# Convolution taps that read their input from PSUM, and one scan in place of four

## The chip, the core and the metric

The kernel runs on one core of a Trainium2 chip. The metric is the device time of one execution in microseconds, and lower is better. A span is the time from the first to the last recorded instruction of one profiled execution.

## What is computed

Two transformer blocks follow each other on one sequence of 512 tokens with 1024 channels, all in float32. The first block has a gated delta rule over four heads of 128; its q, k and v are projections of the normed input, put through a causal depthwise convolution of width 4 and SiLU:

```python
qkv = jax.nn.silu(causal_dwconv(jnp.concatenate([q, k, v], axis=-1), conv_w))   # width 4, zeros ahead of the first token
q, k, v = jnp.split(qkv.astype(jnp.float32), 3, axis=-1)
q = l2norm(q.reshape(hs))
k = l2norm(k.reshape(hs))
```

It ends with an MLP and a gated projection. The second block has an mLSTM over four heads beside a latent attention. The mLSTM's q and k come through a convolution of the same kind with a bias, and its forget gates through a log sigmoid and a running sum over the sequence:

```python
qk_ml = jax.nn.silu(causal_conv(qk_ml, conv_w, conv_b))                         # width 4
logf = jax.nn.log_sigmoid(chunk(f_pre).astype(f32))
b = jnp.cumsum(logf, axis=-1)
```

## The kernel before

Activations lie transposed, 128 channels on the partitions and 512 tokens along the free dimension, so a convolution over tokens is a sum of four shifted copies of a row, each times a number per partition. Every weight matrix is read in blocks of 128 by 1024 or the like. A block lands by DMA in one of three `raw` buffers; ScalarE writes its rounded upper part to `wh` (line 2325), GpSimd the residual to `wl` in two halves (line 1912), and TensorE multiplies each slice three times (`wh` and `wl` with the upper part of the activations, `wh` with their lower part, lines 1954 to 1956, or 984 to 986 where tokens lie on the partitions).

The order of all work is written out by hand. `plan()` lists the tiles; each is one GEMM into one of four PSUM banks, in turn. TensorE may start tile t when tile t - 4 has been read: it waits on `bank_read["act"]` or `bank_read["dve"]`, and `Plan.READER` says which engine counts for which kind of tile. Four more banks, `aux`, hold sums, transposes and small products. On ScalarE, `tile()` reads a tile and then splits the weight blocks whose slot is free by then (`split`); on VectorE, `tile()` waits for a GEMM, `freed` counts the bank as read, and `link` makes the next instruction wait for this one.

The first block's tiles are kn 0 to 3 (the keys), q 0 to 3, v 0 to 3, hp 0 and 1, ch 0 and 1, and so on. `HEADS` numbers the twelve convolutions: 0 to 3 keys, 4 to 7 q, 8 to 11 v. For keys, VectorE multiplies the tile by the norm factor into `craw` (`keys`, line 2705). For q and v, ScalarE copies the tile to `craw` (line 2429) and then writes the last tap to `cc` from the bank (line 2430), which frees it. VectorE adds the other three taps from `craw`, which has three zeros ahead of column 3 (`conv`, line 2750), and ScalarE applies SiLU (`conv_silu`, line 2439). `craw` and `cc` have two buffers each. Between the convolutions stand, on TensorE, the squared sums of the heads (line 2130) and the transposes of keys and v (line 2024); on VectorE, `kd` and `bv` (lines 2792 and 2804) read these transposes, and the `AT` tiles (line 2815) are made ahead of the gram matrices (lines 2168 and 2170), which wait for the last `bv`.

The second block begins with tiles gates2 and qk2 0 to 2, then v2 (0,0) to (0,3), qk2 3, and v2 (1,0) to (1,3). VectorE scales qk2 j by the norm factor `nrow` into `craw2` (`scaled_qk`), which frees the bank; ScalarE writes the last tap from `craw2` to `cc2`; VectorE adds three taps (line 1565). Between scaling and taps stand the forget gates: `lf`, four scans of 128 tokens each chained by their last column (line 1555), `nbs`, and later `c4`, the running maximum `m4` (line 1579), its splitting into `r4h` and `r4l`, and `em`. VectorE's order there is gates2, `scaled_qk(0)`, the forget gates, `ncol`, `scaled_qk(1)`, `conv(0)`, `scaled_qk(2)`, the maxima, `conv(1)`, `conv(2)`, `scaled_qk(3)`, `conv(3)`.

The functions that the diff touches, and what calls them:

## Time and profile before

| | |
|---|---|
| three runs | 1385.59, 1385.69, 1387.89 us; median 1385.69 |
| the profiled execution's own time | 1383.27 us |
| its span | 1381.5 us, mean granted TensorE clock 0.984 |
| TensorE busy | 1321.5 us (96%), 6265 matmuls |
| VectorE busy | 608.5 us (44%) |
| ScalarE busy | 527.0 us (38%) |
| GpSimd busy | 570.0 us (41%) |

Busy time is a share of the whole span, an average over stages with different limits. A matmul row's length is longer than the distance to the next one, since matmuls overlap; starts are the better ruler. Idle time of an engine other than TensorE says nothing by itself; what counts is whether TensorE waits.

### The profile page before, as it was taken

The page shows a single profiled execution, that of the slowest core. Times are in us where ns is not written, and L with a number is a line of the kernel's source. Part 1 is how long each engine was busy: PE and PEld are TensorE (multiplying, and loading weights), DVE is VectorE, ACT ScalarE, POOL GpSimd, SP SyncE. Part 2 cuts the span into 40 slices and gives each one's busy share as a digit, 9 for nine tenths or more (in the row PEclk, how much of TensorE's full clock was granted, in tenths as well). Part 3 has the DMA queues.
Part 4 walks back from the last instruction along what each step waited for, and adds up shares of the span by engine and source line. Part 5 has one row for each costly group of instructions (what it writes and reads, how often), then busy time and mean ns, then how long its engine had stood idle before and what let it go on. Part 6 is the DMA issues. An engine that isn't in the chain of part 4 may idle for free.

```text
span 1381.5 us, 15973 instructions
## 1 busy us (share of the span) xinstructions
PE 1321.5 (96%) x6265; PEld 1050.3 (76%) x6265; DVE 608.5 (44%) x847; ACT 527.0 (38%) x814; POOL 570.0 (41%) x429
## 2 busy tenths in 40 slices
PE   7999889999999999999999999989989999999997
PEld 5768778787888888888887865555768888888886
DVE  4967652335115421121376546466468513314123
ACT  5585323535222222221354434545445313323232
POOL 4334232254554554554554342211326544444440
PEclk9999999999999999999999999999999999999998
DMA  6422101232333333333332231100214333333321
GB/s 185 145 57 74 38 16 33 60 107 75 116 92 94 104 92 106 93 93 87 111 92 79 75 74 48 46 16 31 61 46 128 101 92 95 104 92 95 103 61 61
DMA packets 211665, 113.29 MB, mean 82 GB/s; under 512 B 17204, under 2 KB 209536, under 8 KB 211336
## 3 DMA queue, kind: packets, MB, share of 16 engines
q1 hardware_dynamic: 210488, 109.32, 27.9%
q10 hardware_dynamic: 976, 2.90, 0.6%
q8 instruction: 50, 0.82, 0.2%
q14 instruction: 23, 0.19, 0.0%
q0 software_dynamic: 128, 0.07, 0.0%
HBM read 110.16 MB, written 2.11 MB: 81 GB/s over the span
## 4 chain that ended last, share of the span: by engine, by line
PE 82%; DVE 6%; ACT 3%; POOL 1%; issue 1%; DVEq 0%; ACTq 0%
PE bank L1954 21%; PE bank L1956 21%; PE bank L1955 21%; PE aux L2202 1%; PE aux L2218 1%; PE bank L1106 1%; PE aux L1122 1%; PE aux L2231 1%; PE aux L1035 1%; POOL wl L1912 1%; PE aux L1954 1%; PE bank L984 1%; PE aux L1047 1%; PE bank L2002 1%; PE bank L986 1%
## 5 line engine op out<-in xcount | busy, mean ns | idle before, releaser
L1912 POOL TENSOR_TENSOR wl<-raw,wh 128x512 fp32r<-128x512 f32 (+1 forms) x402 | 548.0, 1387 | 748.0 <-ACT wh L2325 747.9
L1954 PE MATMUL bank<-ah,wh 128*128 128x512 f32 x888 | 355.7, 401 | 6.1 <-ACT cc L2430 3.4
L2325 ACT CAST wh<-raw 128x1024 fp32r<-128x1024 f32 (+1 forms) x201 | 208.2, 1038 | 370.2 <-PE bank L1956 358.1
L1956 PE MATMUL bank<-al,wh 128*128 128x512 f32 x888 | 347.8, 392 | 0.0
L1955 PE MATMUL bank<-ah,wl 128*128 128x512 f32 x888 | 347.7, 392 | 0.0
L1954 PEld LDWEIGHTS bank<-ah,wh 128*128 128x128 f32 x888 | 168.1, 189 | 45.9 <-issue 10.5
L1956 PEld LDWEIGHTS bank<-al,wh 128*128 128x128 f32 x888 | 167.8, 189 | 35.5
L1955 PEld LDWEIGHTS bank<-ah,wl 128*128 128x128 f32 x888 | 168.0, 189 | 35.0 <-issue 1.5
L1954 PE MATMUL bank<-yh,wh 128*128 128x512 f32 x488 | 190.6, 391 | 0.1
L1956 PE MATMUL bank<-yl,wh 128*128 128x512 f32 x488 | 190.0, 389 | 0.0
L1955 PE MATMUL bank<-yh,wl 128*128 128x512 f32 x488 | 189.9, 389 | 0.0
L1954 PEld LDWEIGHTS bank<-yh,wh 128*128 128x128 f32 x488 | 91.6, 188 | 19.2 <-DVE yl L2623 0.5
L1956 PEld LDWEIGHTS bank<-yl,wh 128*128 128x128 f32 x488 | 91.6, 188 | 19.1
L1955 PEld LDWEIGHTS bank<-yh,wl 128*128 128x128 f32 x488 | 91.6, 188 | 18.8
L873 DVE TENSOR_TENSOR y<-bank,sg 128x512 f32<-128x512 f32 x22 | 15.2, 692 | 166.5 <-PE bank L1956 161.1
L1794 DVE CAST yh<-y 128x512 fp32r<-128x512 f32 x32 | 34.7, 1085 | 77.7 <-ACT y L1483 77.7
L1809 DVE TENSOR_TENSOR acc<-bank,acc 128x512 f32<-128x512 f32 x23 | 15.9, 692 | 99.3 <-PE bank L1956 99.3
L915 DVE TENSOR_TENSOR x<-bank,x 128x512 f32<-128x512 f32 x24 | 16.6, 692 | 97.7 <-PE bank L1956 97.7
L1479 ACT ACTIVATE rl<-bank 128x512 f32<-128x512 f32 x32 | 19.1, 598 | 92.6 <-PE bank L1956 90.6
L1795 DVE TENSOR_TENSOR yl<-y,yh 128x512 fp32r<-128x512 f32 x32 | 52.2, 1630 | 1.1
L804 ACT ACTIVATE sg<-bank 128x512 f32<-128x512 f32 x22 | 13.2, 599 | 95.5 <-PE bank L1956 90.7
L2750 DVE SCALAR_TENSOR_TENSOR cc<-craw,par,cc 128x512 f32<-128x512 f32 x36 | 36.8, 1028 | 4.7 <-ACT cc L2430 3.3
(452 smaller groups left out, 1645.8 us busy)
## 6 DMA issues: line engine op xcount, KB each, us to landing
raw<-in_w_up SPq DMA_DIRECT2D x54, 512.0 KB, 3.9
raw<-in_w_down SPq DMA_DIRECT2D x48, 512.0 KB, 4.1
raw<-in_w_in SPq DMA_DIRECT2D x39, 512.0 KB, 3.9
raw<-in_w_gate SPq DMA_DIRECT2D x22, 512.0 KB, 3.8
raw<-in_w_out SPq DMA_DIRECT2D x16, 512.0 KB, 3.8
raw<-in_ple_gate SPq DMA_DIRECT2D x8, 512.0 KB, 3.9
raw<-in_w_down SPq DMA_DIRECT2D x8, 384.0 KB, 3.3
xtok<-in_x SPq DMA_DIRECT2D x4, 512.0 KB, 5.2
```

The lines of the kernel that those rows point to most:

```text
L873: freed(nc.vector.tensor_tensor(y, ps, sg[:, i % 3, :], ALU.mult))
L915: freed(nc.vector.tensor_tensor(x[:, m, :], ps, x[:, m, :], ALU.add))
L1479: tile("up2", (c, j), lambda ps: nc.scalar.activation(rl[:, :], ps, ACT.Relu))
L1794: link(nc.vector.tensor_copy(yh[c % 2][:, j, :], y))
L1795: nc.vector.tensor_tensor(yl[c % 2][:, j, :], y, yh[c % 2][:, j, :].bitcast(F32), ALU.subtract).then_inc(y_ready[1], 1)
L1809: freed(nc.vector.tensor_tensor(acc[:, m, :], ps, acc[:, m, :], ALU.add))
L1912: nc.gpsimd.tensor_tensor(wl[pl.slot[b]][:, half], raw[b % RAW][:, half], wh[pl.slot[b]][:, half].bitcast(F32), ALU.subtract).then_inc(wl_ ...
L1954: nc.tensor.matmul(ps, h[:, c:c + P], mh[:, k, :], start=(n == 0), stop=False)
L1955: nc.tensor.matmul(ps, l[:, c:c + P], mh[:, k, :], start=False, stop=False)
L1956: last = nc.tensor.matmul(ps, h[:, c:c + P], ml[:, k, :], start=False, stop=(n == nk - 1))
L2325: nc.scalar.copy(wh[pl.slot[b]][:, 0:w], raw[b % RAW][:, 0:w]).then_inc(wh_ready, 1)
L2750: i = nc.vector.scalar_tensor_tensor(c[:, :], r[:, tap:tap + T], g_of("conv_qkv", 12 * tap + conv_tile(j)), c[:, :], ALU.mult, ALU.add)
```

## The change

For q and v, ScalarE's copy to `craw` goes; it only writes the last tap from the bank. VectorE's three taps read the bank, each on a shorter stretch (tap 2 from column 1 of `cc` on, tap 1 from column 2, tap 0 from column 3), in place of the zeros ahead of the row. VectorE frees the bank with the last tap, so q and v are in `READER` as VectorE's. Keys are as before.

In the second block VectorE multiplies each qk2 bank by `nrow` in place, ScalarE writes the last tap from the bank, VectorE's taps read the bank and the last one frees it; `craw2` and its zeros go. The four chained scans become one over 512 tokens: its state is the sum of `lf` and the state, then the minimum of that and `lf`, which leaves the running sum as it is because no `lf` is above zero.

```diff
--- before.py
+++ after.py
@@ -177,7 +177,7 @@
-    READER = dict(kn="dve", q="act", v="act", hp="act", ch="dve", cc="dve", cb="dve", z="act", wout="dve",
+    READER = dict(kn="dve", q="dve", v="dve", hp="act", ch="dve", cc="dve", cb="dve", z="act", wout="dve",
                   gate="act", up="dve", down="dve", proj="act", pgate="act", gates2="dve", qk2="dve", v2="act",
@@ -357,7 +357,6 @@
         mrn = sb("mrn", [P, T])
-        craw2 = [sb(f"craw2{i}", [P, 3 + T], at=offs["qf"] + i * 2080) for i in range(2)]
         cc2 = [sb(f"cc2{i}", [P, T], at=offs["qf"] + 4160 + i * 2048) for i in range(2)]
@@ -509,7 +508,6 @@
         cols_loaded = signal("cols_loaded")
-        pads_zero = signal("pads_zero")
         alog_exp = signal("alog_exp")
@@ -524,7 +522,6 @@
         pt_ready = signal("pt_ready")
-        pads2_zero = signal("pads2_zero")
         pos_loaded = signal("pos_loaded")
@@ -539,7 +536,7 @@
         em_ready = signal("em_ready")
-        conv2_done = signal("conv2_done")
+        qk_scaled = signal("qk_scaled")
         silu2_ready = signal("silu2_ready")
@@ -663,6 +660,12 @@
             return aux[k % 6] if k < 4 or k > 5 else bank[k - 2]
+        def convolved(eng, j):
+            if j < H:
+                eng.wait_ge(conv_done, j + 1)
+            else:
+                evacuated(eng, *HEADS[j])
+
         def conv_tile(j):
@@ -1261,15 +1264,15 @@
             def conv_evac(j):
                 if j >= 2:
-                    act.wait_ge(conv2_done, j - 1)
+                    evacuated(act, "qk2", j - 2)
                     act.wait_ge(silu2_ready, j - 1)
                 tile("qk2", j)
+                act.wait_ge(qk_scaled, j + 1)
+                nc.scalar.activation(cc2[j % 2][:, :], bank[pl.at["qk2", j] % NBANK][:, :], ACT.Copy,
+                                     scale=g_of("conv_w_2", 12 + j)).then_inc(last_tap, 1)
+
+            def conv_silu(j):
                 evacuated(act, "qk2", j)
-                nc.scalar.activation(cc2[j % 2][:, :], craw2[j % 2][:, 3:3 + T], ACT.Copy,
-                                     scale=g_of("conv_w_2", 12 + j)).then_inc(last_tap, 1)
-
-            def conv_silu(j):
-                act.wait_ge(conv2_done, j + 1)
                 dst = (q2 if j < 2 else k2)[:, j % 2, :]
@@ -1531,15 +1534,10 @@
         def vector_second(dve, link, tile, freed, lower, norm_fill, add_square):
-            for i in range(2):
-                nc.vector.memset(craw2[i][:, 0:3], 0.0).then_inc(pads2_zero, 1)
             def scaled_qk(j):
                 ps = tile("qk2", j)
-                if j >= 2:
-                    dve.wait_ge(conv2_done, j - 1)
-                    dve.wait_ge(last_tap, H + j - 1)
-                freed(nc.vector.tensor_tensor(craw2[j % 2][:, 3:3 + T], ps, nrow[:, :], ALU.mult))
+                nc.vector.tensor_tensor(ps, ps, nrow[:, :], ALU.mult).then_inc(qk_scaled, 1)
             ps = tile("gates2", 0)
@@ -1550,23 +1548,19 @@
             link(nc.vector.scalar_tensor_tensor(lf[:, :], g2[:, :], 0.0, lf[:, :], ALU.min, ALU.subtract))
-            for c in range(NC):
-                s = slice(c * P, (c + 1) * P)
-                link(nc.vector.tensor_tensor_scan(bs[:, s], ones[0:8, :], lf[:, s],
-                                                  bs[:, c * P - 1:c * P] if c else 0.0, ALU.mult, ALU.add))
+            link(nc.vector.tensor_tensor_scan(bs[:, :], lf[:, :], lf[:, :], 0.0, ALU.add, ALU.min))
             nc.vector.tensor_scalar(nbs[:, :], bs[:, :], -1.0, None, ALU.mult).then_inc(forget_sums_ready, 1)
             def conv(j):
-                r, c = craw2[j % 2], cc2[j % 2]
-                dve.wait_ge(pads2_zero, 2)
-                evacuated(dve, "qk2", j)
-                dve.wait_ge(last_tap, H + j + 1)
+                ps, c = bank[pl.at["qk2", j] % NBANK], cc2[j % 2]
+                dve.wait_ge(last_tap, 3 * H + j + 1)
                 for tap in (2, 1, 0):
-                    i = nc.vector.scalar_tensor_tensor(c[:, :], r[:, tap:tap + T], g_of("conv_w_2", 4 * tap + j),
-                                                       c[:, :], ALU.mult, ALU.add)
+                    late = 3 - tap
+                    i = nc.vector.scalar_tensor_tensor(c[:, late:T], ps[:, 0:T - late], g_of("conv_w_2", 4 * tap + j),
+                                                       c[:, late:T], ALU.mult, ALU.add)
                     if tap:
                         link(i)
-                i.then_inc(conv2_done, 1)
+                freed(i)
             dve.wait_ge(ncol_ps, 1)
@@ -2414,7 +2408,7 @@
                 if j >= 2:
-                    act.wait_ge(conv_done, j - 1)
+                    convolved(act, j - 2)
                     act.wait_ge(silu_ready, j - 1)
@@ -2425,13 +2419,12 @@
                 act.wait_ge(gemm_done, t + 1)
-                act.wait_ge(pads_zero, 1)
-                nc.scalar.copy(craw[j % 2][:, 3:3 + T], bank[t % NBANK][:, :])
-                tile(kind, h, lambda ps: nc.scalar.activation(cc[j % 2][:, :], ps, ACT.Copy, scale=tap))
+                nc.scalar.activation(cc[j % 2][:, :], bank[t % NBANK][:, :], ACT.Copy, scale=tap).then_inc(last_tap, 1)
+                tile(kind, h)
             def conv_silu(j):
                 kind, h = HEADS[j]
-                act.wait_ge(conv_done, j + 1)
+                convolved(act, j)
                 if kind == "v" and h >= 2:
@@ -2710,7 +2703,7 @@
             nc.vector.memset(pin[:, 0, 0:16], 0.0)
-            nc.vector.memset(pin[:, 1, 0:16], 0.0).then_inc(pads_zero, 1)
+            nc.vector.memset(pin[:, 1, 0:16], 0.0)
             dve.wait_ge(ab_ps, 1)
@@ -2742,17 +2735,20 @@
             def conv(j):
                 r, c = craw[j % 2], cc[j % 2]
-                if j < H:
-                    dve.wait_ge(last_tap, j + 1)
-                else:
-                    evacuated(dve, *HEADS[j])
+                ps = tile(*HEADS[j]) if j >= H else None
+                dve.wait_ge(last_tap, j + 1)
                 for tap in (2, 1, 0):
-                    i = nc.vector.scalar_tensor_tensor(c[:, :], r[:, tap:tap + T],
-                                                       g_of("conv_qkv", 12 * tap + conv_tile(j)), c[:, :],
+                    late = 3 - tap if j >= H else 0
+                    src = ps[:, 0:T - late] if j >= H else r[:, tap:tap + T]
+                    i = nc.vector.scalar_tensor_tensor(c[:, late:T], src,
+                                                       g_of("conv_qkv", 12 * tap + conv_tile(j)), c[:, late:T],
                                                        ALU.mult, ALU.add)
...
                         link(i)
-                i.then_inc(conv_done, 1)
+                if j < H:
+                    i.then_inc(conv_done, 1)
+                else:
+                    freed(i)
             def head_norm(j):
```

## Rows read from the trace of the kernel before

**Rows 1.** The page of the whole run, its part 1: busy us (share) x instructions.

```profile
PE 1321.5 (96%) x6265; PEld 1050.3 (76%) x6265; DVE 608.5 (44%) x847; ACT 527.0 (38%) x814; POOL 570.0 (41%) x429
```

**Rows 2.** TensorE's waits, whole run: us in total, times, longest us.

```profile
PE bank L1954 <- ACT cc L2430: 3.4, 1, 3.4
...
PE bank L1954 <- POOL wl L1912: 1.9, 1, 1.9
...
PE bank L984 <- POOL wl L1912: 1.0, 1, 1.0
```

**Rows 3.** The answers for lines 2750 and 2661: duration ns min/median/max, first and last start.

```profile
L2750 DVE SCALAR_TENSOR_TENSOR cc<-craw,par,cc x36: 715/752/1828, 52.3 to 117.4; 128x512 f32<-128x512 f32 x36
...
L2661 DVE SCALAR_TENSOR_TENSOR zl<-aux,par,zh x6: 741/747/752, 12.2 to 22.2; 128x512 fp32r<-128x512 f32 x6
```

**Rows 4.** Timeline of VectorE, first block: start us, us, line, operation, tiles, count.

```profile
55.32 2.32 DVE L2750 SCALAR_TENSOR_TENSOR cc<-craw,par,cc 128x512 f32<-128x512 f32 x3
...
87.97 3.20 DVE L2750 SCALAR_TENSOR_TENSOR cc<-craw,par,cc 128x512 f32<-128x512 f32 x3
...
114.35 3.79 DVE L2750 SCALAR_TENSOR_TENSOR cc<-craw,par,cc 128x512 f32<-128x512 f32 x3
...
119.62 0.68 DVE L2804 TENSOR_TENSOR bv<-aux,gT 128x512 f32<-128x512 f32 x1
```

**Rows 5.** Timeline of TensorE around the first GEMM of v.

```profile
70.06 0.47 PE L1954 MATMUL bank<-ah,wh 128*128 128x512 f32 x1 [3.36 <-ACT cc L2430]
...
73.25 0.63 PE L1956 MATMUL bank<-al,wh 128*128 128x512 f32 x1
73.67 0.50 PE L1954 MATMUL bank<-ah,wh 128*128 128x512 f32 x1
74.01 0.39 PE L1955 MATMUL bank<-ah,wl 128*128 128x512 f32 x1
```

**Rows 6.** Timeline of ScalarE ahead of it.

```profile
68.73 0.59 ACT L2429 COPY craw<-bank 128x512 f32<-128x512 f32 x1
69.22 0.69 ACT L2430 ACTIVATE cc<-bank,par 128x512 f32<-128x512 f32 x1
```

**Rows 7.** Timeline of TensorE, v 2 to the gram matrices.

```profile
90.67 0.58 PE L1954 MATMUL bank<-ah,wh 128*128 128x512 f32 x1 [1.85 <-POOL wl L1912]
...
118.85 1.03 PE L2024 MATMUL aux<-cst,vT 128*128 128x128 f32 x8
121.84 1.13 PE L2168 MATMUL aux<-kT 128*128 128x128 f32 x8 [1.95 <-DVE bv L2804]
```

**Rows 8.** Timeline of ScalarE ahead of v 2.

```profile
88.21 1.04 ACT L2325 CAST wh<-raw 128x1024 fp32r<-128x1024 f32 x1
```

**Rows 9.** Two windows: busy of PE, PEld, DVE, ACT, POOL, granted clock, DMA share, GB/s.

```profile
90.00:96.00 6.00, 5.33 (x16) 4.26 (x17) 5.93 (x7) 4.03 (x7) 4.21 (x4) 0.72 0.34 90
120.00:126.00 6.00, 4.16 (x26) 3.77 (x27) 5.08 (x15) 5.27 (x11) 0.00 (x0) 1.00 0.02 5
```

**Rows 10.** Timeline of VectorE, second block.

```profile
754.22 4.07 DVE L1555 TENSOR_TENSOR_SCAN bs<-ones,bs,lf 8x128 f32<-8x128 f32 x3
...
759.87 2.32 DVE L1565 SCALAR_TENSOR_TENSOR cc<-craw,par,cc 128x512 f32<-128x512 f32 x3
...
768.37 4.56 DVE L1565 SCALAR_TENSOR_TENSOR cc<-craw,par,cc 128x512 f32<-128x512 f32 x6
```

**Rows 11.** Timeline of TensorE, second block.

```profile
759.09 1.02 PE L970 MATMUL aux<-g,cst 8*4 8x512 f32 x2
...
767.61 0.28 PE L984 MATMUL bank<-wh,ah 128*128 128x256 f32 x1
...
774.20 0.47 PE L1954 MATMUL bank<-ah,wh 128*128 128x512 f32 x1 [0.67 <-ACT v L1287]
```

**Rows 12.** The chain that ended last, second block: start us, us, engine, tile, line.

```profile
775.15 0.94 ACT wh L2325
776.17 5.03 POOL wl L1912 x4
```

More of the change, by code:

```diff
@@ L1263, in conv_evac @@
                 if j >= 2:
-                    act.wait_ge(conv2_done, j - 1)
+                    evacuated(act, "qk2", j - 2)
                     act.wait_ge(silu2_ready, j - 1)
                 tile("qk2", j)
-                evacuated(act, "qk2", j)
-                nc.scalar.activation(cc2[j % 2][:, :], craw2[j % 2][:, 3:3 + T], ACT.Copy,
+                act.wait_ge(qk_scaled, j + 1)
+                nc.scalar.activation(cc2[j % 2][:, :], bank[pl.at["qk2", j] % NBANK][:, :], ACT.Copy,
                                      scale=g_of("conv_w_2", 12 + j)).then_inc(last_tap, 1)
             def conv_silu(j):
-                act.wait_ge(conv2_done, j + 1)
+                evacuated(act, "qk2", j)
                 dst = (q2 if j < 2 else k2)[:, j % 2, :]
```

## The prediction

> **What bounds the kernel now.** Read the page first: TensorE is busy for 96% of the span [rows 1]. So an edit off TensorE changes the time only where TensorE stands still, or where it is made to. Next comes the list of TensorE's waits, kept to the two places that the change touches [rows 2]: 3.4 us for ScalarE's `cc` before the GEMM of v 0, 1.9 us for a weight residual of GpSimd before v 2, and 1.0 us for one in the second block, beside one of 0.67 us before qk2 3 [rows 11]. The scans have no row there. Then the timelines of these stretches, to see what ends each wait and what would be late next.
>
> A GEMM takes one of four banks, so it waits until the tile four places back has been read. v 0 waits for q 0, v 1 for q 1, v 2 for q 2; in the second block, v2 (0,1) for qk2 0, v2 (0,2) for qk2 1, v2 (0,3) for qk2 2. The change moves the release of exactly these banks from the end of one read to the end of three taps on VectorE.
>
> **Price of a tap.** From SBUF, `cc` and pointer scalar, undisturbed: 752 ns median, and 2.32 us for three in a row [rows 3, 4]. The nearest row with one operand in PSUM and a pointer scalar is the `zl` operation, 747 ns [rows 3]. I take 2.32 us for three taps from PSUM; bounds are 2.2 us (a little shorter operand, 509 to 511 columns) and 2.5 us (an unseen PSUM start cost). The upper end also covers this: the Trainium skill, "VectorE: DVE Perf Modes", section "Rules for kernel authors", advises copying a matmul's output to SBUF first when many operations follow, and its errata section charges a PSUM source 62 cycles more than an SBUF one; by it, as an estimate, each hold would last 0.2 us longer and the sum below rise by about 0.4 us. The trace's 747 against 752 ns does not show that surcharge for two-input operations.
>
> Beside GpSimd the SBUF taps are dearer: the longest took 1828 ns [rows 3], and conv 11 needed 3.79 us for three [rows 4]. The operation with a PSUM operand has a maximum of 752 ns. So 2.32 us holds there too, a saving of 1.4 us for conv 11.
>
> **First block, v 0.** ScalarE now copies q 0 (from 68.73) and then scales it (69.22, 0.69 us, ends 69.91); TensorE starts at 70.06, 0.15 us later [rows 5, 6]. New: the copy goes, the scaling runs 68.73 to 69.42, the taps 69.45 to 71.77, TensorE starts at 71.92. That is 1.86 us late; what ScalarE saves (0.49 us) is inside it. After the present wait the matmuls start 0.43 us apart until 73.67, then 0.23 us: TensorE at 1.2 GHz, then at 2.4 GHz [rows 5]. If the slow stretch ends at the same instant, the longer wait takes the place of some slow matmuls: before, nine matmuls started ahead of 73.67, now (73.67 - 71.92) / 0.43 = four, and the other five cost 5 x 0.23 = 1.1 us. If it lasts as long after the restart as before, the delay stays 1.86. I take 1.5.
>
> **First block, v 2.** Everything up to the key transposes follows TensorE, so it moves by 1.5. conv 6 starts behind `kd` 0 and 1, at 87.97 [rows 4], new 89.47, and frees q 2's bank at 91.79; TensorE starts at 91.94 instead of 90.67 [rows 7], 1.27 late. What it waits for today, the cast at 88.21 and the residual behind it [rows 8], moves by 1.5 less two saved copies (0.98), by 0.5, and is no longer last. The weight wait goes and a bank wait comes. The clock is open here. Today nine matmuls are slow after a wait of 1.85, which costs 8 x 0.2 = 1.6 us (granted 0.72 of full speed from 90 to 96); a wait of 1.95 at 121.84 left it at 1.00 [rows 7, 9]. The new wait is about 1.6 us. If the clock stays up, TensorE gains at most the 1.27 back, for then the head sums wait for ScalarE's squares: these stand behind silu 7, so behind conv 7, which VectorE reaches after conv 6 and two more `kd` at about today's time.
>
> **First block, the gram matrices.** Today they wait for `bv` 3, on a chain of VectorE: conv 11, eight `AT` tiles, `bv` 2, four tiles, `bv` 3 [rows 4]. conv 11 1.4 us shorter looks like that gain, but `bv` 2 needs the transposes that TensorE starts at 118.85 [rows 7]; the first four end about 119.4, `bv` 2 starts at 119.62. So 0.3 us is gained, and the transposes are late next. First block in all: 1.27 - 0.3 = +1.0 with the slow clock, -0.3 without. The rows split evenly; I take +0.4.
>
> **Second block, the hold.** conv 0 ends at 759.87 + 2.32 = 762.2 [rows 10]; v2 (0,1), 24 matmuls of 0.12 us ahead of v2 (0,2), needs it at 764.7: hidden. conv 1 is queued behind the scaling of qk2 2, the `c4` copy, the maximum scan and the splitting of maxima, and starts at 768.37. It frees qk2 1's bank at 768.37 + 2.28 = 770.65, but v2 (0,2) starts at 767.61 today [rows 11]. It will start at 770.80, 3.19 late. conv 2 follows at once and ends at 772.9, when v2 (0,3) is not yet due: hidden. A wait of 3.2 us is like that of 3.4 us before v 0, behind which the clock fell; I take the same 1.6 us on top (bounds 0 and 3.2). v2 (0,3) then ends 4.8 us late. Of that some is given back: today the casts wait behind four v2 reads that are queued behind silu 2, so the next cast starts at 775.15 on the chain [rows 12], 1.6 us after the last v2 matmul; new it starts some 0.55 us after it. The chain from there (cast, four halves on GpSimd, v2 (1,0) at 781.24) moves as a whole: 4.79 - 1.05 = +3.7. With the clock up it is +2.1. The 0.67 us wait before qk2 3 [rows 11] is inside the same slack.
>
> The scaling in place writes PSUM, which no VectorE row of before does. Four operations, two of them (qk2 1, qk2 2) ahead of conv 1. The same multiplication into SBUF takes 0.69 us; I take that, with bounds of 0.6 and 1.7 us (the dearest contended 512-column rows are near this), so -0.2 to +2.0 on the path.
>
> **The scan and the rest.** Four scans, the last three of them 4.07 us [rows 10], become one over 512 columns. It is worth 3 to 4 us to VectorE, and nothing to the end: the next thing is the copy of `ncol`, which waits for TensorE's small matmuls behind the GEMM of qk2 2, and the matmuls that use the sums start at 759.09 without a wait [rows 11]. The cover is the qk2 2 GEMM; were it gone, the 3 to 4 us would count. If one scan took as long as four, nothing changes. The memsets of the pads, three columns each, and eight ScalarE copies (0.59 us each [rows 6]) lie beside GEMMs, but for the two already counted. No DMA is issued anew or moved past another; the weight ring follows the GEMMs. The new wait of VectorE for the GEMM is over before its `last_tap` wait is.
>
> **Sum.** +0.4 + 3.7 = +4.1 us. The profiled execution took 1383.27 us (span 1381.5) and would take 1387.4; the median of the runs shown is 1385.69, 2.4 us above it, and I forecast from that: 1389.8 us.
>
> **Rivals.**
> - A, the holds bind but the clock is kind (0.22): +2.1 in the second block, -0.3 to +0.4 in the first: +1.8 to +2.5, 1388. For it: the wait of 1.95 us that left the clock up. Against: the clock did fall after the waits of 3.4 and 1.9 us [rows 5, 9].
> - B, faster (0.06): VectorE's relief decides. If conv 1 ended by 767.5, 3.1 us before it is due by my rows, the second block would cost nothing, and the first could give 1.6 for the clock and 0.3 at the gram matrices: -1.9, 1383.8. It would take the maximum scan chain to start earlier, but it hangs on `ncol` and `cb_ps` of TensorE. A rule of the Trainium skill points this way: "SBUF — State Buffer", section "SBUF: two separate sides", has a VectorE operation with two SBUF inputs shut GpSimd out for its whole length, and the reverse. The long taps agree; but what is freed this way stands off TensorE's chain.
> - C, costlier (0.10): the in-place write or taps from PSUM are slow, or the clock is half for twice as long: +6 to +8, 1392 to 1393.5. For it: no such row. Against: `zl` at 747 ns.
> - The forecast (0.62): +2.8 to +6, 1388.5 to 1391.5.
>
> **How the numbers follow.** 0.2% is 2.8 us, about what a measurement of this kernel tells from no change. Slower by more: C and most of the forecast, with a little of A: 0.66. Within it: A and the low edge of the forecast: 0.28. Faster: B: 0.06. The range takes A's low end with the spread of the runs (1386.3) and C's near end (1392.8).
>
> **What would show it.** In the profile after: (1) a wait of about 5 us before v 0, ended by VectorE's tap; (2) before v 2 a bank wait in place of GpSimd's; (3) a new wait of about 3.2 us at line 984's third tile, ended by a tap of conv 1, the largest single item, with granted clock below 1.00 behind it; (4) taps of j from 4 on at about 750 ns, none over 1000; (5) VectorE idle ahead of `ncol` where the scans were. The prediction fails if (3) is absent, if taps from PSUM run far off 750 ns, or if slow clock stretches elsewhere shift by more than two.

## Result: 1389.79 us, 0.22% slower

The changed kernel took 1389.79 us (median of 20 runs, 1387.4 to 1392.53), the kernel before beside it on the same chip 1385.8 us (20 runs, 1382.49 to 1391.52). The ratio is 1.0022, 95% interval [1.0012, 1.0032]: 4.0 us by the medians, 3.0 us by the ratio. Six of the 20 runs of the kernel before took 1390.59 to 1391.52 us and the other 14 at most 1387.89; the changed kernel's runs have no such gap. The total is the forecast's. How it is made up is not, as the profile and the experiments show.

The profiled execution of the changed kernel took 1391.37 us with a span of 1389.5 us. That is 8 us more than that of before (1381.5), twice what the medians differ by, so this pair of profiles must not be read as if all of its difference were the change.

Part 1 of its page, in the form of [rows 1]:

```profile
PE 1323.2 (95%) x6265; PEld 1052.3 (76%) x6265; DVE 599.2 (43%) x842; ACT 522.9 (38%) x806; POOL 567.0 (41%) x429
```

VectorE and ScalarE have less to do (9.3 and 4.1 us); TensorE is as busy as before. TensorE's waits, kept to those that matter (us in total, times, longest):

```profile
PE bank L1948 <- DVE cc L2743: 6.9, 2, 5.3
PE aux L1050 <- DVE st L1634: 4.9, 2, 3.2
...
PE bank L987 <- POOL wl L1906: 0.9, 1, 0.9
...
PE aux L2124 <- ACT hsq L2469: 0.5, 1, 0.5
```

That a bank stays taken until VectorE's last tap is called a hold below, whether TensorE has to wait for it or not. Both waits of the first block now end on VectorE's tap: 5.3 us before v 0 and 1.6 before v 2, in place of 3.4 for ScalarE and 1.9 for GpSimd [rows 2]. The second block has no wait for a tap. A wait for `st` (line 1640 before) has grown to 3.2 us, at a place the change doesn't touch.

The rows of the taps, the scaling in place and the scan (duration ns min/median/max, first and last start):

```profile
L2743 DVE SCALAR_TENSOR_TENSOR cc<-bank,par,cc x24: 740/748/749, 70.3 to 118.5; 128x511 f32<-128x511 f32 x8, 128x510 f32<-128x510 f32 x8, 128x509 f32<-128x509 f32 x8
L2743 DVE SCALAR_TENSOR_TENSOR cc<-craw,par,cc x12: 714/752/1823, 53.1 to 69.2; 128x512 f32<-128x512 f32 x12
L1559 DVE SCALAR_TENSOR_TENSOR cc<-bank,par,cc x12: 741/749/752, 763.9 to 789.6; 128x511 f32<-128x511 f32 x4, 128x510 f32<-128x510 f32 x4, 128x509 f32<-128x509 f32 x4
```

```profile
L1540 DVE TENSOR_TENSOR bank<-bank,nrow x4: 690/696/700, 753.5 to 786.3; 128x512 f32<-128x512 f32 x4
```

```profile
L1551 DVE TENSOR_TENSOR_SCAN bs<-lf x1: 2211/2211/2211, 756.9 to 756.9; 8x512 f32<-8x512 f32 x1
```

None of 36 taps from PSUM took over 752 ns; only keys, still read from SBUF, show 1823. GpSimd worked beside several of them; its two residual halves from 96.67 to 99.22 us cover the whole of the tap that starts at 97.56 and took 742 ns. Scaling in place costs what scaling into SBUF did (0.69), and one scan takes 2.2 us.

TensorE's timeline from v 0 to v 2, answering to [rows 5, 7]:

```profile
72.81 0.77 PE L1948 MATMUL bank<-ah,wh 128*128 128x512 f32 x1 [5.29 <-DVE cc L2743]
...
78.06 0.63 PE L1948 MATMUL bank<-ah,wh 128*128 128x512 f32 x1
78.49 0.52 PE L1949 MATMUL bank<-ah,wl 128*128 128x512 f32 x1
78.85 0.39 PE L1950 MATMUL bank<-al,wh 128*128 128x512 f32 x1
...
81.17 1.02 PE L2124 MATMUL aux<-hsq,ones 128*128 128x512 f32 x2
...
94.36 0.47 PE L1948 MATMUL bank<-ah,wh 128*128 128x512 f32 x1 [1.59 <-DVE cc L2743]
...
100.59 0.70 PE L2124 MATMUL aux<-hsq,ones 128*128 128x512 f32 x1 [0.54 <-ACT hsq L2469]
```

After v 0's start thirteen matmuls go by 0.43 us apart before the spacing shrinks at 78.49, 5.7 us at the lower clock, called a slow stretch below; before it was 3.6 us, nine matmuls [rows 5]. At v 2 the reverse: no slow matmul follows. The windows of both blocks (busy of PE, PEld, DVE, ACT, POOL, granted clock, DMA share, GB/s):

```profile
90.00:96.00 6.00, 3.97 (x25) 3.05 (x23) 5.22 (x8) 3.82 (x7) 2.50 (x2) 1.00 0.02 4
...
763.00:769.00 6.00, 6.00 (x19) 2.86 (x19) 5.59 (x9) 4.33 (x5) 0.79 (x1) 0.65 0.37 107
769.00:775.00 6.00, 6.00 (x42) 5.96 (x41) 5.80 (x8) 0.35 (x1) 2.28 (x2) 0.78 0.32 87
```

The first was 0.72 before [rows 9]. The other two show the clock down in the second block, beside matmuls, with no wait. TensorE's timeline there, and VectorE's:

```profile
764.91 1.91 PE L975 MATMUL aux<-bs,cst 8*4 8x512 f32 x2
766.75 0.58 PE L987 MATMUL bank<-wh,ah 128*128 128x256 f32 x1
767.13 0.42 PE L988 MATMUL bank<-wl,ah 128*128 128x256 f32 x1
767.34 0.41 PE L989 MATMUL bank<-wh,al 128*128 128x256 f32 x1
...
774.76 0.36 PE L987 MATMUL bank<-wh,ah 128*128 128x256 f32 x1
```

```profile
763.27 0.16 DVE L1566 COPY ncol<-aux 128x4 f32<-128x4 f32 x1 [2.82 <-PE aux L969]
...
772.30 4.54 DVE L1559 SCALAR_TENSOR_TENSOR cc<-bank,par,cc 128x511 f32<-128x511 f32 x6
```

The clock falls inside the small matmuls behind the GEMM of qk2 2 (two take 1.91 us; the pairs ahead take 1.02 and 1.09), and v2 (0,0) and (0,1) then run 0.21 us apart instead of 0.12. So v2 (0,2) is reached only at 774.7, and conv 1, the first half of the six taps that start at 772.30, frees its bank at 774.6: the hold is there and costs nothing on top. The 2.82 us of idle ahead of `ncol` is where the scans were.

VectorE's timeline ahead of the gram matrices, answering to [rows 4]:

```profile
116.90 2.31 DVE L2743 SCALAR_TENSOR_TENSOR cc<-bank,par,cc 128x511 f32<-128x511 f32 x3
119.12 1.66 DVE L2811 TENSOR_SCALAR AT<-GR,gT 128x128 f32<-128x128 f32 x8
122.04 0.69 DVE L2800 TENSOR_TENSOR bv<-aux,gT 128x512 f32<-128x512 f32 x1 [1.26 <-PE aux L2018]
```

conv 11 lost 1.5 us of its 3.79 [rows 4], and VectorE then stands 1.26 us for the transposes.

### The profile page after: what moved, and what is told of

It is laid out like the page before. It is cut to its first block, busy times and chain, and to the rows that moved or that the text cites. A ratio compares the mean times of both kernels' runs of the same rounds, so it can differ in the third digit from the quotient of the medians.

```text
span 1389.5 us, 15955 instructions
## 1 busy us (share of the span) xinstructions
PE 1323.2 (95%) x6265; PEld 1052.3 (76%) x6265; DVE 599.2 (43%) x842; ACT 522.9 (38%) x806; POOL 567.0 (41%) x429
## 4 chain that ended last, share of the span: by engine, by line
PE 82%; DVE 6%; ACT 3%; issue 1%; POOL 1%; DVEq 0%; ACTq 0%
PE bank L1948 21%; PE bank L1950 21%; PE bank L1949 21%; PE aux L2196 1%; PE aux L2212 1%; PE bank L1109 1%; PE aux L1125 1%; PE aux L2225 1%; PE bank L987 1%; PE aux L1050 1%; PE aux L1038 1%; PE aux L1948 1%; PE bank L989 1%; PE bank L988 1%; PE bank L1996 1%
## 5 line engine op out<-in xcount | busy, mean ns | idle before, releaser
L1788 DVE CAST yh<-y 128x512 fp32r<-128x512 f32 x32 | 34.8, 1086 | 77.7 <-ACT y L1486 77.7
L2624 DVE TENSOR_TENSOR rstd<-rstd,sq 128x512 f32<-128x512 f32 x28 | 32.1, 1145 | 4.9 <-ACT sq L2352 4.9
```

The costliest lines, as they stand in the source:

```text
L1788: link(nc.vector.tensor_copy(yh[c % 2][:, j, :], y))
L2624: nc.vector.tensor_tensor(rstd[:, :], rstd[:, :], sq[:, k % 2, :], ALU.add).then_inc(sum_ready, 1)
```

## The experiments

Theory: the loss is the time that the last tap comes later than ScalarE's read, at v 0, v 2 and v2 (0,2). Rivals: one of the three carries it all; or the loss is not in the banks, but in where the clock falls or in what that sets off later. All times:

| kernel | median us (lowest to highest, runs) | ratio to before [95%] |
|---|---|---|
| first block's part alone | 1390.05 (1387.25 to 1391.16, 12) | 1.0020 [1.0006, 1.0034] |
| second block's part alone | 1389.37 (1385.35 to 1392.05, 12) | 1.0012 [0.9996, 1.0028] |
| the scan alone | 1386.42 (1383.48 to 1391.04, 12) | 1.0002 [0.9986, 1.0017] |
| change, conv 1 and 2 early | 1389.49 (1384.35 to 1390.54, 12) | 1.0012 [0.9998, 1.0027] |
| change, queries copied | 1387.37 (1385.62 to 1389.03, 12) | 0.9995 [0.9980, 1.0009] |
| change, both of these | 1387.48 (1385.15 to 1388.38, 12) | 0.9999 [0.9984, 1.0014] |
| before, conv 1 and 2 early | 1386.28 (1382.99 to 1391.64, 12) | 0.9998 [0.9982, 1.0014] |
| before, once more | 1387.56 (1383.17 to 1390.85, 12) | 1.0000 [0.9983, 1.0017] |
| before, cast moved | 1383.56 (1381.05 to 1387.52, 12) | 0.9980 [0.9965, 0.9994] |
| change, both and cast moved | 1382.31 (1379.61 to 1387.16, 12) | 0.9972 [0.9958, 0.9985] |
| change, only q 0 copied | 1386.97 (1384.29 to 1387.91, 12) | 1.0001 [0.9988, 1.0013] |
| change, cast moved | 1386.41 (1384.35 to 1388.52, 12) | 0.9993 [0.9980, 1.0006] |

The first four ran on one chip beside 35 runs of the kernel before (median 1386.47), the next four on another beside 35 (1387.82), the last four on a third beside 35 (1386.00). Ratios are to be compared, not medians of different groups. A difference of two ratios is uncertain by some 0.0017 to 0.0022, 2.4 to 3 us.

**The first block's part alone.** The change's edits of ScalarE's and VectorE's convolution code (lines 2408 to 2427 and 2735 to 2754 of the changed kernel), with `READER` for q and v; the second block as before.

```diff
-    READER = dict(kn="dve", q="act", v="act", ...
+    READER = dict(kn="dve", q="dve", v="dve", ...
...
-                nc.scalar.copy(craw[j % 2][:, 3:3 + T], bank[t % NBANK][:, :])
-                tile(kind, h, lambda ps: nc.scalar.activation(cc[j % 2][:, :], ps, ACT.Copy, scale=tap))
+                nc.scalar.activation(cc[j % 2][:, :], bank[t % NBANK][:, :], ACT.Copy, scale=tap).then_inc(last_tap, 1)
+                tile(kind, h)
```

> Only the first block's part of the change: taps of q and v from PSUM; the second block and its four scans as before. Theory (holds in both blocks): v 0 waits about 5.2 us in place of 3.4, v 2 for a tap of conv 6, the gram matrices come 1.5 us later than before, and the median is +0.4 to +2.5 us over the kernel before, ratio about 1.001. Rival 1 (the first block carries it all, since the changed kernel's profile has no wait ahead of the second block's third v2 tile): the full +4 us, ratio 1.003. Rival 2 (nothing in the first block counts, relief of VectorE beside GpSimd pays for the holds): 1.000 or below.

Measured: 1.0020, 2.8 us, as much as the whole change within the error and just above the 0.4 to 2.5 us expected. The waits are those of the changed kernel (6.9 us in two, the longest 5.3).

**The second block's part alone**, `vector_second` and `conv_evac` of the change, with the four scans kept.

```diff
-                freed(nc.vector.tensor_tensor(craw2[j % 2][:, 3:3 + T], ps, nrow[:, :], ALU.mult))
+                nc.vector.tensor_tensor(ps, ps, nrow[:, :], ALU.mult).then_inc(qk_scaled, 1)
...
-                i.then_inc(conv2_done, 1)
+                freed(i)
```

> Only the second block's taps from the scaled bank; four scans and the first block as before. Theory: v2 (0,2) can't start before the third tap of conv 1 plus 0.15 us, 12.2 to 12.3 us after the copy of ncol starts, whatever the clock did before it; where the clock stayed up there is a wait of about 3.2 us ended by the tap, where it fell in the small matmuls the wait is short or absent. Median +2 to +3.7 us, ratio about 1.002. Rival 1 (the hold is hidden, the changed kernel was slow there by its clock alone): no wait even with the clock up, ratio 1.000.

Measured: 1.0012, its interval from nothing to twice that. Of the profiles with held banks in their old order it is the only one that shows the hold as a wait. TensorE's waits, its timeline and its windows:

```profile
PE bank L984 <- DVE cc L1559: 1.3, 1, 1.3
```

```profile
770.62 0.36 PE L984 MATMUL bank<-wh,ah 128*128 128x256 f32 x1 [1.34 <-DVE cc L1559]
```

```profile
763.00:769.00 6.00, 6.00 (x41) 6.00 (x39) 5.77 (x8) 1.64 (x2) 2.97 (x2) 0.72 0.10 19
769.00:775.00 6.00, 4.66 (x40) 4.48 (x38) 3.60 (x5) 2.55 (x5) 0.00 (x0) 1.00 0.23 69
```

v2 (0,2) starts at 770.62 instead of 767.61 [rows 11], 3.0 us late where the prediction had 3.19. Only 1.34 of it is a wait; the rest went into slow matmuls ahead of it (0.72 from 763 to 769, against 1.00 in before). Behind the wait the clock stayed at 1.00. What is left of the 3.0 us when the forget gates are spread (line 1057 before; 794.98 against 792.94) is 2.0 us, near the 2.1 of the prediction's case "with the clock up".

**The scan alone.**

```diff
-            for c in range(NC):
-                s = slice(c * P, (c + 1) * P)
-                link(nc.vector.tensor_tensor_scan(bs[:, s], ones[0:8, :], lf[:, s], ...
+            link(nc.vector.tensor_tensor_scan(bs[:, :], lf[:, :], lf[:, :], 0.0, ALU.add, ALU.min))
```

> Only the one scan in place of four. Theory: VectorE is done 2 to 3 us earlier and then idles until the small matmuls behind the GEMM of qk2 2, nothing else moves: 1.000, within 0.1%. Rival (the earlier end is passed on): up to -3 us, 0.998. Rival (less of VectorE beside TensorE's small matmuls lets the clock fall there more often): +1 us.

Measured: 1.0002, nothing. Its profile has a span of 1381.8 us and the waits of before.

**The change with conv 1 and conv 2 ahead of the maxima**, so that their banks come free earlier.

```diff
             scaled_qk(2)
+            conv(1)
+            conv(2)
             dve.wait_ge(cb_ps, 1)
...
-            conv(1)
-            conv(2)
             scaled_qk(3)
```

> The changed kernel, but conv 1 and conv 2 stand ahead of the c4 copy, the maximum scan and the splitting on VectorE. Theory: the banks of qk2 1 and 2 are free before v2 (0,2) and v2 (0,3) are due, the second block costs nothing against before and gains up to 1 us, for SiLU 2 and so the v2 reads and the weight casts come earlier; the mixer's maxima are later by 4.6 us and hidden. Median -2 to -4.5 us against the changed kernel, that is 1.000 to 1.001 of the kernel before. Rival (the hold was no cost): same as the changed kernel, 1.002 to 1.003. Rival (the late maxima are passed on): slower than the changed kernel.

Measured: 1.0012 against the change's 1.0022, and both intervals hold both values; 1.4 us less where 2 to 4.5 were expected, and not told from nothing. In its profile the six taps start at 764.92 instead of 772.30, so the hold is gone, yet the spread comes no earlier than in the changed kernel: the clock was at 0.50 from 763 to 769. The slow stretch took what the hold would have.

**The change with the queries copied by ScalarE as before** (v and the second block still read in PSUM). It takes away the holds before v 0 and v 2.

```diff
+                if kind == "q":
+                    nc.scalar.copy(craw[j % 2][:, 3:3 + T], bank[t % NBANK][:, :])
+                    tile(kind, h, lambda ps: nc.scalar.activation(cc[j % 2][:, :], ps, ACT.Copy, scale=tap))
+                    return
```

> The changed kernel, but the four q tiles are copied by ScalarE and their banks freed as before; only v is read from PSUM by the taps. Theory: v 0 waits 3.4 us again and v 2 for GpSimd's residual as before, the gram matrices start at 121.5 to 121.9, the 0.3 us of the shorter conv 11 is kept; the median falls by 1 to 2 us against the changed kernel, 1.001 to 1.002 of the kernel before, what is left being the second block's. Rival (the first block's hold is nothing but clock luck): as the changed kernel, 1.002 to 1.003.

Measured: 0.9995, 0.0027 or 3.7 us below the change, more than the 1 to 2 us expected. The waits before v 0 and v 2 are again 3.4 us for ScalarE and 1.8 for GpSimd. So the first block's holds carry most of the cost, if not all of it.

**Both: queries copied and the taps early.**

> Both holds undone and the rest of the change kept: q copied by ScalarE, v and qk2 read from PSUM, conv 1 and 2 ahead of the maxima, one scan. Theory (the two holds are the whole cost): 0.999 to 1.000 of the kernel before, mean 2 to 4 us below the changed kernel. Rival (a third place, VectorE beside GpSimd at the latent norms, is what makes the difference): stays 1 us or more above the kernel before, with a wait of about 3.2 us for st there.

Measured: 0.9999. Beside the queries copied alone (0.9995) the early taps gain nothing that the times show, where the forecast's 3.7 us for the second block would be 0.0027.

**The kernel before with conv 1 ahead of `scaled_qk(2)` and conv 2 behind it**, both ahead of the maxima.

```diff
+            conv(1)
             scaled_qk(2)
+            conv(2)
             dve.wait_ge(cb_ps, 1)
```

> The kernel before with conv 1 and conv 2 ahead of the maxima, all taps from SBUF. Theory: SiLU 2, the v2 reads and the weight casts come earlier, the waits of 0.7 and 1.0 us around qk2 3 shrink, the maxima are hidden: 0 to -1 us, ratio 0.999 to 1.000. Rival (the clock falls in the small matmuls and takes it back): 1.000 to 1.001.

Measured: 0.9998, nothing; here no tap holds a bank.

**The kernel before once more**, with no edit.

> The kernel before itself, once more as a kernel of its own. It measures what two equal kernels differ by. All theories: 1.000, within 0.1%. In its profile: if the clock stays up just ahead of the latent norms, GpSimd's subtraction meets VectorE's cast of ckh there (1.4 us in place of 0.43) and TensorE waits about 3.2 us for st; if it falls there, not.

Measured: 1.0000 by the times, but its profiled span is 1385.8 us, 4.3 us above the one that the prediction used. 1.6 us of it arises between the gram matrices and the state products (line 2242) and 0.5 around the forget gates, where slow stretches of the clock fell elsewhere; 2.3 behind the spread, where the second block's latent norms stand. The last hi cast of `latent_norms`, the subtraction behind it, GpSimd's residuals (start, us) and TensorE's wait for `st` in the new trace:

```profile
L1620 DVE CAST ckh<-cq x1: 1397/1397/1397, 859.2 to 859.2; 128x512 fp32r<-128x512 f32 x1
L1621 DVE TENSOR_TENSOR ckl<-cq,ckh x1: 1671/1671/1671, 860.6 to 860.6; 128x512 fp32r<-128x512 f32 x1
```

```profile
858.68 3.08 POOL L1912 TENSOR_TENSOR wl<-raw,wh 128x512 fp32r<-128x512 f32 x2 [9.05 <-ACT wh L2325]
```

```profile
PE aux L1047 <- DVE st L1640: 4.9, 2, 3.2
```

and the same in the first trace of the kernel before:

```profile
L1620 DVE CAST ckh<-cq x1: 426/426/426, 856.0 to 856.0; 128x512 fp32r<-128x512 f32 x1
L1621 DVE TENSOR_TENSOR ckl<-cq,ckh x1: 693/693/693, 856.5 to 856.5; 128x512 fp32r<-128x512 f32 x1
```

```profile
856.59 3.00 POOL L1912 TENSOR_TENSOR wl<-raw,wh 128x512 fp32r<-128x512 f32 x2 [9.02 <-ACT wh L2325]
```

```profile
PE aux L1047 <- DVE st L1640: 1.9, 2, 1.7
```

The traces show a race between two engines. In the first trace the cast starts at 856.01 and GpSimd's residual at 856.59; in the second the residual starts at 858.68, ahead of the cast at 859.2, which then takes 1.40 us instead of 0.43, and `ckl` behind it 1.67 instead of 0.69. Everything behind them on VectorE is late, and TensorE stands 3.2 us. The changed kernel's profile has this too (the 3.2 us row above), and so have seven of the eight traces of the experiments so far (waits of 2.9 to 3.2 us; the scan alone has it not); so a part of the 8 us between the first two profiles is not the change. The Trainium skill, "SBUF — State Buffer", section "SBUF: two separate sides", has VectorE operations in a two-port mode or with two SBUF inputs and GpSimd's exclude each other for a whole instruction, whichever starts first; both lengths and the order of starts agree with it.

**The kernel before with the three hi casts on ScalarE**, which shortens VectorE's chain and takes the cast away from that race. VectorE's three scalings now come ahead of the three subtractions, no longer in turn with them. The last lines shown stand in ScalarE's code.

```diff
-                    link(nc.vector.scalar_tensor_tensor(c, c, gain, wt[...], ALU.mult, ALU.mult))
-                    link(nc.vector.tensor_copy(hi, c))
-                    nc.vector.tensor_tensor(lo, c, hi.bitcast(F32), ALU.subtract).then_inc(cq_ready, 1)
+                    nc.vector.scalar_tensor_tensor(c, c, gain, wt[...], ALU.mult, ALU.mult).then_inc(pads2_zero, 1)
+                for j in range(3):
+                    dve.wait_ge(alog_exp, j + 2)
+                    nc.vector.tensor_tensor(lo, cq[:, j, :], hi.bitcast(F32), ALU.subtract).then_inc(cq_ready, 1)
...
+                for j in range(3):
+                    act.wait_ge(pads2_zero, j + 3)
+                    nc.scalar.copy(cqh[:, j, :] if j < 2 else ckh[:, 0, :], cq[:, j, :]).then_inc(alog_exp, 1)
```

> The kernel before with one edit elsewhere: in the latent norms of the second block (around 850 to 870 us) the cast of each normed tile to the matmul's type is a copy on ScalarE and no longer on VectorE. Theory L (in the runs whose clock stays up at 849 us, the last cast ran beside GpSimd's subtraction and took 1.40 instead of 0.43 us, the exps of og came later, and TensorE waited 3.2 us for VectorE's st; which of these two a run gets depends on where the clock falls, and this is one source of the scatter of equal kernels): no cast of 1.4 us, no wait of 3.2 us for st, about 1.5 to 2.5 us less than before where the collision happened, so a ratio of 0.9985 to 0.9995 and a narrower spread of the runs. Rival (ScalarE's three copies come later than VectorE's, or the wait was only covering another one): ratio 1.000, with a wait for the latent tiles or for og in its place.

Measured: 0.9980 [0.9965, 0.9994], 2.8 us by the ratio, a little more than the 1.5 to 2.5 expected. Twelve runs still spread over 6.5 us, against 7.7 for twelve of the unchanged kernel, so no narrower spread is shown; that half of the theory has nothing for it. In its trace (the cast, then the wait):

```profile
L1316 ACT CAST ckh<-cq x1: 622/622/622, 859.7 to 859.7; 128x512 fp32r<-128x512 f32 x1
L1625 DVE TENSOR_TENSOR ckl<-cq,ckh x1: 683/683/683, 860.8 to 860.8; 128x512 fp32r<-128x512 f32 x1
```

```profile
PE aux L1047 <- DVE st L1644: 1.7, 1, 1.7
```

**The change with the queries copied, the taps early and the casts on ScalarE.**

> The version put together from the runs so far: the change, with the first block's query tiles copied out by ScalarE as before, the second block's convolutions 1 and 2 ahead of the maxima, and the cast of the latent norms on ScalarE. If the first block's holds are what the change costs and the latent cast is worth 1.5 to 2.5 us: 1385 us beside a before of 1387, a ratio of 0.998 to 0.999, and 2 us under the version with copied queries. If the latent cast is worth nothing: ratio 1.000, as the version with copied queries had it (0.9999).

Measured: 0.9972 [0.9958, 0.9985], 1382.31 us: faster than both kernels. It isn't told apart from the kernel before with the cast moved (0.9980): what is gained over the kernel before comes with the cast.

**The change with only q 0 copied.** Its bank is the one that v 0 waits for; v 2's is still held by a tap.

```diff
+                if j == H:
+                    nc.scalar.copy(craw[j % 2][:, 3:3 + T], bank[t % NBANK][:, :])
+                    tile(kind, h, lambda ps: nc.scalar.activation(cc[j % 2][:, :], ps, ACT.Copy, scale=tap))
+                    return
```

> The change, with only query tile 0 of the first block copied out by ScalarE; its bank is the one that values tile 0 waits for. Queries 1 to 3 are still read in PSUM, so the bank of values tile 2 is still held. Theory H0 (the 5.3 us hold before values tile 0 carries the loss in block 1, the 1.6 us hold before values tile 2 little): wait before v 0 is 3.4 us and ends on ScalarE, v 2 still waits 1.6 us for VectorE; 1.5 to 2.3 us less than the changed kernel, so about 1.0005 to before. Theory H2 (the holds count alike or v 2's counts more): within 1 us of the changed kernel, ratio 1.0015 to 1.003.

Measured: 1.0001 [0.9988, 1.0013]; 0.0021 or 2.9 us below the change (expected 1.5 to 2.3), the two intervals just touching. TensorE's waits, of which v 0's is back to ScalarE and v 2's still stands:

```profile
PE bank L1949 <- ACT cc L2425: 3.5, 1, 3.5
...
PE bank L1949 <- DVE cc L2751: 1.6, 1, 1.6
```

One copy of 0.59 us gives back all that can be measured. And in its stretch the wait before v 2 is a gain: with it the clock was 1.00 from 90 to 96 us in all five profiles that have it, while GpSimd's wait of 1.8 to 1.9 us, in the other nine, is followed by 0.72 (0.77 in one). From v 0's head sums to the gram matrices the five took 43.1 us, the nine 44.6 to 44.9. The times don't show this gain: with all queries copied, so without this wait, the ratio is 0.9995, with it 1.0001.

**The change with the cast moved.**

> The changed kernel with the latent norms' cast on ScalarE. The hold of the banks is untouched. If the latent collision is independent of the change: 1.5 to 2.5 us less than the changed kernel, and still 2 to 4 us more than the kernel before with the same edit. If the change's loss came in truth through the later collision: no difference left between this kernel and the kernel before with the same edit.

Measured: 0.9993, that is 0.0013 above the kernel before with the same edit (1.8 us, by the intervals uncertain by some 2.6; the medians, here of one group, are 2.9 us apart) and 0.0029 or 4.0 us below the change, where 1.5 to 2.5 were expected. That fits effects that stand side by side. That a part of the loss came through the later collision isn't excluded: the unchanged kernel collides in one of its two traces, and how often each kernel does isn't known.

**All fourteen profiles together.** One profile has its slow stretches where chance put them. The last matmul ahead of v 0, before which no edit does more than leave out a few columns of zeros, already starts anywhere from 65.0 to 67.1 us. So here are distances between starts of TensorE's rows, averaged over the kernels that are alike at the place: the last matmul ahead of v 0, v 0, the head sums behind it, the first gram matrices, the first state products (line 2242), the `ncol` matmuls (line 966), the spread (line 1057), and the first matmul of line 1975 (at 1012.15 in before). All lines are those of the kernel before.

| stretch | with (profiles) | without | us |
|---|---|---|---|
| ahead of v 0 to v 0: q 0's bank held | 5.7 (4) | 3.8 (10) | +1.9 |
| v 0 to head sums: same | 8.1 (4) | 7.6 (10), 6.9 to 8.5 | +0.5 |
| head sums to gram matrices: q 2's bank held | 43.1 (5) | 44.7 (9) | -1.6 |
| gram matrices to state products: q 0's bank held | 109.2 (4) | 108.5 (10), 107.5 to 110.8 | +0.7 |
| `ncol` to spread: qk2 held, old order | 36.9 (5), 36.8 to 37.1 | 35.7 (5), 34.8 to 36.9 | +1.2 |
| same: qk2 held, taps early | 35.3 (3), 33.8 to 36.9 | 35.7 (5) | -0.4 |
| spread to line 1975: cast moved | 217.1 (3) | 220.9 (11) | -3.8 |

From line 1975 to the end all took 369.3 or 369.4 us. Added up, the change comes to +1.9 + 0.5 - 1.6 + 0.7 + 1.2 = +2.7 us (times: +3.0), its first block alone to +1.5 (+2.8), its second alone to +1.2 (+1.7), with only q 0 copied to -0.4 (+0.1), with the queries copied to +1.2 (-0.7), with the taps early to +1.1 (+1.7). Each time is uncertain by 1.4 to 2.2 us, and none contradicts its sum; the sum for the queries copied lies just at the edge of its interval. Of the rows, +1.9 and -1.6 are clear of their scatter. The +0.5, the +0.7 and the second block's +1.2 are not: there the slow stretches alone make the values without a hold differ by 1.5 to 3.2 us.

## Why the prediction was right, and where it was not

**The total** was forecast at +4.1 us and 1389.8; measured were +4.0 by the medians, +3.0 by the ratio, and 1389.79. That banks held by taps make the kernel slower was right. That the total met the forecast so closely was luck: two terms erred in opposite directions, the first block's +0.4 and the second's +3.7, and the base of 1385.69, the median of three runs, lay near that of twenty (1385.8) though single runs differ by 9 us.

**Price of a tap, of the scaling in place, of conv 11.** Right: 748, 696 ns and 2.31 us, beside 752, 692 and 2.32. The surcharge for a PSUM source that a page of the Trainium skill has ("VectorE: DVE Perf Modes", errata section) is not there for these two-input operations. The same page's advice to copy first when many operations follow (section "Rules for kernel authors") turned out right for q 0, for a reason that it doesn't give: the copy frees the bank.

**First block, v 0.** The wait and the 1.86 us later start were right (5.29; 1.93 by the table). The step that failed is "I take 1.5": I let part of the slow stretch pass during the longer wait and had 1.86 as the most. In the traces no shortening is seen: the slow stretch lasted 5.2 to 5.7 us behind the longer wait, and 3.1 to 6.1 us in the ten traces with a wait of 3.4 to 3.5 (8.10 against 7.62 us to the head sums on the average). So 2.4 us are lost there instead of 1.5, of which 1.9 is clear of the scatter. The number of slow matmuls behind an equal wait varied by itself: v 0 to the head sums took 7.16 us in one trace of the kernel before and 8.29 in the other. The Trainium skill, "TensorE: Matmul & The Clock Gate", Part 1, says that the same kernel shows different numbers of slow matmuls from run to run; the traces agree.

**First block, v 2.** The bank wait of 1.59 us (forecast 1.6) and the cap by ScalarE's squares (0.54 us of wait at the head sums) came as told. The clock, for which I had split evenly, stayed up each time. That makes this stretch a gain of 1.6 us, near the 1.8 of the forecast's kind case (from +1.5 to -0.3, conv 11 and the transposes included). VectorE stood for the transposes, as told. In place of the block's +0.4 stands +0.8 at the gram matrices, and +1.5 at the state products: between the two the slow stretch of the clock fell in a dearer place in all four profiles with q 0's bank held, and in half of the others, which can be chance. I had no term for that. The time of the first block alone, +2.8 us [+0.8, +4.7], leaves +0.4 out.

**Second block.** The step that failed most is that v2 (0,2) starts 3.19 us late with the clock falling behind it, +3.7 in all. The hold has its size: 3.0 us late and 2.0 left in the trace that shows it. But in most traces a slow stretch lies across the small matmuls and v2 (0,0), and then v2 (0,2) is reached when conv 1 has freed its bank or nearly. I had taken the clock of the one trace read (1.00 there) for the kernel's; two of the five traces with the second block as before have the long stretch as well (36.8 and 36.9 us from `ncol` to the spread). With held banks it takes 36.8 to 37.1 in all five: by these ten traces the hold takes away the lucky cases and leaves the others as they were, +1.2 us on the average, not +3.7. The time of the second block alone (+1.7, at most +3.9) doesn't exclude +3.7; that the early taps gained 1.4 us in one pair and nothing in the other speaks against it. I named the absence of the 3.2 us wait as what would make the prediction fail. In the profile after it is absent, so by its own sign this part did fail; the total stood because the first block cost more.

**Scan, pads, ScalarE's copies.** The scan is right at nothing, by the kernel with the scan alone and by the idle 2.82 us ahead of `ncol`. The pads and the copies were not run alone.

**Rivals.** A (kind clock) had +2.1 for the second block, near the 2.0 of the one trace that waits there, but -0.3 to +0.4 for the first, which cost more. B (faster) fell: VectorE's relief of 9 us moved nothing that the times show. C fell with the prices. That slow stretches shift elsewhere, which I named as what would upset the forecast, did happen, and with the collision it is most of what the two first profiles differ by beyond the medians.

**What stays open.** The sum of the averages and the times agree only within about two microseconds, so how the three parts share the loss is known no better than that. That GpSimd's wait of 1.8 us and VectorE's of 1.6 differ in what follows them was seen, five against nine, but not what in them decides. Why the cast's move gains 3.8 us of profile where the collision alone is worth 2.0 (the two traces without it took 219.2 us from the spread to line 1975, the nine with it 221.2) wasn't separated; with the edit VectorE's chain is shorter there even without a collision. What sets the remaining spread of 6.5 us between equal runs isn't known either. The profiled run of the kernel before with the cast moved points at the clock: it is one of that kernel's three slowest (1386.96 to 1387.52, the other nine at most 1384.51), and between the gram matrices and the state products it took 110.8 us, against 107.5 to 109.2 in the other thirteen traces.

## What to carry to other kernels

Reading operands in PSUM saves a copy and lengthens the hold of the bank by every operation that reads it; ask of each bank which GEMM takes it next and whether that GEMM is due, and copy out just the tiles (here one of eight) whose successor is already waiting. Before costing a difference of two profiles, take a second profile of the unchanged kernel: here equal kernels differed by 4.3 us. And look through such pairs for operations whose length jumps (0.43 to 1.40 us): here it was a race between two engines, and the edit that took it out gained 2.8 us, about what the whole change lost.

## What the runs showed of the hardware

- VectorE operations with one operand in PSUM and a pointer scalar take 740 to 752 ns for some 510 columns, beside GpSimd's work too (742 ns for the one at 97.56 us in the profile after); from SBUF taps reach 1823 ns. Writing in place in PSUM costs nothing extra (696 ns for 512 columns).
- A one-input cast of 512 columns on VectorE took 426 ns alone and 1397 ns when GpSimd's subtraction had started 0.5 us ahead of it (the two traces of the kernel before).
- Behind a wait of 5.3 us the matmuls ran at half clock for 5.2 to 5.7 us (four traces), behind one of 3.4 to 3.5 us for 3.1 to 6.1 (ten). Behind waits of 1.6 us at one place the clock stayed up five times of five; behind 1.8 to 1.9 us at the same place it fell nine times of nine (0.72 to 0.77 of full speed from 90 to 96 us).
- The clock also fell where TensorE was busy with small matmuls and waited for nothing (764.9 us in the profile after).
